# Samples in quarters, inputs first, and two weight places used once: a one-core trunk step with a mixture of experts

## What is computed

```python
x = _layernorm(x, ln_in_g, ln_in_b)
mix, C, n, m, S = _mixer(x, C_in[l], n_in[l], m_in[l], S_in[l], w_in[l], ...)
...
h = jnp.concatenate([h_a, h_b], axis=-1).astype(x.dtype)
return h @ w_out_l, C, n, m, S
```

## Time and profile before

| | us |
|---|---|
| median of the runs | 1262.06 |
| profiled execution, in all | 1263.85 |
| its span, first to last instruction | 1262.0 |
| TensorE matmul busy | 1166.6 (92%) |
| VectorE busy | 400.7 (32%) |
| ScalarE busy | 178.2 (14%) |
| GpSimd busy | 77.2 (6%) |
| mean granted TensorE clock | 0.976 |
| bytes moved | 441.92 MB, 350 GB/s over the span |

### The profile page before, as it was taken

One profiled execution on the slowest core, in us unless ns is written; L12 is line 12 of the kernel. 1 busy time (PEld: TensorE's weight loads), 2 busy tenths in 40 slices (PEclk: granted clock), 3 DMA queues, 4 the chain that ended last, 5 costly groups with the idle time before them and its releaser, 6 DMA issues.

```text
span 1262.0 us, 13214 instructions
## 1 busy us (share of the span) xinstructions
PE 1166.6 (92%) x5599; PEld 483.0 (38%) x5599; DVE 400.7 (32%) x643; ACT 178.2 (14%) x321; POOL 77.2 (6%) x77
## 2 busy tenths in 40 slices
PE   3999999799999997899999999999999999998984
PEld 2777774643333332242333333332323232322221
DVE  6866423841223130112322222232323222214115
ACT  1253242411010110020101010100101010110001
POOL 3100141400101030000000000000000000000000
PEclk9999999899999998999999999999999999999987
DMA  9562111579999999999999999999999999999891
GB/s 313 176 180 67 67 68 67 208 300 420 421 421 421 422 420 386 421 422 421 416 422 421 421 421 421 406 422 420 421 420 421 420 422 412 422 421 413 370 420 55
DMA packets 70029, 441.92 MB, mean 350 GB/s; under 512 B 7824, under 2 KB 7856, under 8 KB 20816
## 3 DMA queue, kind: packets, MB, share of 16 engines
q1 hardware_dynamic: 65168, 425.52, 82.6%
q0 software_dynamic: 4800, 15.51, 3.7%
HBM read 436.28 MB, written 4.73 MB: 349 GB/s over the span
## 4 chain that ended last, share of the span: by engine, by line
PE 70%; DMA 19%; DVE 8%; ACT 2%; issue 1%; SPq 1%; DVEq 0%
PE ps L935 41%; DMA more<-in_w_up 11%; PE ps L543 9%; PE ps L919 5%; PE ps L871 3%; DVE y_s L1740 2%; PE ps L761 2%; DMA ring<-in_w_gate 2%; DMA more<-in_w_down 2%; DMA more<-in_w_gate 2%; PE ps L926 1%; PE ps L571 1%; DVE h_s L1738 1%; ACT hTe L1084 1%; DMA ring<-in_w_up 1%; PE ps L951 1%
## 5 line engine op out<-in xcount | busy, mean ns | idle before, releaser
L935 PE MATMUL ps<-ring,xTe 128*64 128x512 f32 x1536 | 357.4, 602 | 13.4 <-DMA ring<-in_w_up 9.1
L935 PEld LDWEIGHTS ps<-ring,xTe 128*64 128x64 f32 x1536 | 103.9, 136 | 242.0 <-issue 241.8
L1722 DVE TENSOR_TENSOR xs<-xs,ps 128x512 f32<-128x512 f32 (+1 forms) x128 | 70.5, 551 | 365.3 <-PE ps L919 364.7
L935 PE MATMUL ps<-ring,hTe 128*64 128x512 f32 x768 | 181.4, 613 | 4.5 <-DMA ring<-in_w_down 4.5
L935 PE MATMUL ps<-more,xTe 128*64 128x512 f32 x512 | 117.1, 598 | 6.0 <-DMA more<-in_w_up 5.8
L543 PE MATMUL ps<-xT,ring 128*128 128x288 f32 x448 | 116.6, 417 | 1.0 <-PE ps L543 0.6
L935 PEld LDWEIGHTS ps<-ring,hTe 128*64 128x64 f32 x768 | 51.7, 139 | 119.7 <-issue 119.4
L543 PEld LDWEIGHTS ps<-xT,ring 128*128 128x128 f32 x448 | 85.8, 196 | 25.6 <-issue 2.3
L919 PE MATMUL ps<-y_s,GT 128*128 128x512 f32 (+1 forms) x256 | 81.8, 518 | 1.2 <-ACT y_s L1084 1.2
L1738 DVE TENSOR_SCALAR h_s<-ps 128x512 f32<-128x512 f32 x32 | 21.8, 681 | 159.3 <-PE ps L935 159.3
L1754 DVE TENSOR_TENSOR ple<-ple,ps 128x512 f32<-128x512 f32 (+1 forms) x64 | 35.3, 551 | 105.0 <-PE ps L871 90.8
(11 more groups left out here) (344 smaller groups left out, 796.2 us busy)
## 6 DMA issues: line engine op xcount, KB each, us to landing
ring<-in_w_gate SPq DMA_DIRECT2D x96, 1024.0 KB, 10.7
ring<-in_w_up SPq DMA_DIRECT2D x96, 1024.0 KB, 12.1
ring<-in_w_down SPq DMA_DIRECT2D x96, 1024.0 KB, 13.6
more<-in_w_gate SPq DMA_DIRECT2D x32, 1024.0 KB, 12.2
more<-in_w_up SPq DMA_DIRECT2D x32, 1024.0 KB, 12.1
more<-in_w_down SPq DMA_DIRECT2D x32, 1024.0 KB, 13.8
ring<-in_w_in SPq DMA_DIRECT2D x28, 512.0 KB, 6.1
ring<-in_w_out SPq DMA_DIRECT2D x8, 512.0 KB, 5.0
```

The lines of the kernel that those rows point to most:

```text
L935: last = mm(ps[64 * q:64 * q + 64, bank0 + half, :], lhs(k, q), wide(t)[:, k % 2, half * 512:(half + 1) * 512], start=False, stop=k == KT - 1)
L1722: last = tt(xs[0:r, i, c], xs[0:r, i, c], new, ALU.add)
```

## The change

- *Samples in quarters.* The samples' tile becomes `xq`, [128, 256]: partition 32q + t has quarter q of sample t. Its adds, statistics, normalisations and the share of the embeddings are done in that form. Statistics of the four quarters have to be brought together: VectorE spreads them with a mask (`spread_stats`) and TensorE multiplies by a matrix that is one where partitions agree modulo 32 (`row_stats`). Gains are loaded once more in quarters, eight small loads each time. The router product of the samples runs on a copy of them repeated four times (`xT4`), the selection on all 128 partitions. The bf16 parts of the samples are made in quarters, by ScalarE and VectorE, and put back into rows by 12 small products (`sample_rows`).
- *Inputs first.* SyncE loads all of x, then the first columns of the constants (the identity), then the gains; the other constants follow the first group of w_in. GpSimd's first loads wait until x is in. The statistics of all tiles are taken ahead of the wait for the gains.
- *Order.* `x1` stays in natural order (the router weights are loaded to match, in pieces of 128 bytes), and the reordering is done by ScalarE in `part` and by GpSimd in `rest`. TensorE does the prompt's part of the ranks ahead of the samples' rows, and both prompt-state blocks behind the ranks. The first `OH` is made in halves. The first six outputs on GpSimd's queue go ahead of its state operations, and those wait for the use of tile 8.
- *Places.* `once0` lies over `T1` and `T2`, `once1` over `V`. Tiles 8 and 9, the first two up tiles of pair 0, go there; from tile 10 on the eight places rotate as before, two tiles later. Tiles 10 to 17 wait for the use of tiles 0 to 7.
- *End.* The last `add_shares` takes a tile's statistics as soon as its adds are done.

The diff, cut to its core:

```diff
-PLACES = (0, 1, 2, 3, 4, 5, 6, 7)
-NWIDE = len(PLACES)
+NWIDE, NONCE = 8, 2
...
-        xs = sb("xs", [P, 3, D])
+        xs, xq = sb("xs", [P, 2, D]), sb("xq", [P, QW])
+        lnq, ln_q = sb("lnq", [P, 4, 6]), sb("ln_q", [P, 2, QW])
...
+        once = [nc.alloc_sbuf_tensor_at(f"once{n}", [P, 2, D], F32, offset=place[b][0]) for n, b in enumerate(("T1", "V"))]
...
+        def place_of(t):
+
+
+            return t if t < NWIDE + NONCE else (t - NONCE) % NWIDE
...
+            for i in range(2):
+                sp.dma_start(xs[:, i, :], x_src[i]).then_inc(S[f"x_in{i}"], 16)
+            for q, x in enumerate(quarters(x_src[2])):
+                sp.dma_start(xq[q * NS:(q + 1) * NS, :], x).then_inc(S["x_in2"], 16)
+            sp.dma_start(cf[:, 0:CF_FIRST], a["const_f"][:, 0:CF_FIRST]).then_inc(S["ident_in"], 16)
+            for n, v in enumerate(("ln_in_g", "ln_in_b")):
+                sp.dma_start((ln_g, ln_b)[n][:, :], a[v].partition_broadcast(P)).then_inc(S["ln1_in"], 16)
+                for q in range(4):
+                    sp.dma_start(ln_q[q * NS:(q + 1) * NS, n, :],
+                                 a[v][q * QW:(q + 1) * QW].partition_broadcast(NS)).then_inc(S["ln1_in"], 16)
...
+                if t < NWIDE + NONCE:
+                    if t == 6:
                         return sp.wait_ge(S["x_norm"], 6)
-                    if place_n == 7:
+                    if t == 7:
                         return sp.wait_ge(S["router_mm"], 3)
-                    return sp.wait_ge(S["slots_used"], range(2 * place_n + 1, PRE, RING)[-1] + 1)
-                p, u = divmod(t - NWIDE, PER)
+                    if t == 8:
+                        return sp.wait_ge(S["out_mm"], 6)
+                    if t == 9:
+                        return sp.wait_ge(S["st_mm"], 2)
+                    return sp.wait_ge(S["slots_used"], range(2 * t + 1, PRE, RING)[-1] + 1)
+                p, u = divmod(t - NWIDE if t >= 2 * NWIDE + NONCE else t - NWIDE - NONCE, PER)
...
+            for n, c0 in enumerate(W_GROUPS):
+                if n == 1:
+                    sp.dma_start(cf[:, CF_FIRST:], a["const_f"][:, CF_FIRST:]).then_inc(S["const_in"], 16)
...
+            pool.wait_ge(S["x_in2"], 64)
...
+                load_quarters("ln1_g", "ln1_b")
...
-                nc.gpsimd.tensor_tensor(out, out if q else x1[0:r, i, :], p, ALU.subtract).then_inc(S["rest_ok"], 1)
-
-            for i in range(3):
+                out = rests[:, i, :]
+                nc.gpsimd.tensor_tensor(natural(out), natural(out if q else x1[:, i, :]), by_row(xb[:, i, q, :]),
+                                        ALU.subtract).then_inc(S["rest_ok"], 1)
...
+            for i in range(2):
                 for q in range(2):
                     rest(i, q)
...
-            pool.wait_ge(S["out_mm"], 6)
...
+            pool.wait_ge(S["slots_used"], PRE + KT - 2 + 1)
...
+            pool.wait_ge(S["x_norm"], 6)
+            load_quarters("ln2_g", "ln2_b")
...
+            def row_stats(n):
+
+                pe.wait_ge(S["lnq_ok"], n)
+                mm(ps[:, STAT_BANK, 0:24], cf[:, CF_SAME:CF_SAME + P], lnq[:, :, :].rearrange("p q s -> p (q s)"),
+                   start=True, stop=True).then_inc(S["lnq_mm"], 1)
...
                 for k in range(KT):
-                    last = mm(ps[0:r, ROUTE_BANKS[i], 0:NE], xT[:, k, t0:t0 + r], w_r[:, k, :],
-                              start=k == 0, stop=k == KT - 1)
+                    x = xT[:, k, t0:t0 + r] if i < 2 else xT4[:, k, :, :].rearrange("p q t -> p (q t)")
+                    last = mm(ps[:, ROUTE_BANKS[i], 0:NE], x, w_r[:, k, :], start=k == 0, stop=k == KT - 1)
...
+            def prompt_ranks():
+
+
+                pe.wait_ge(S["pick_ok"], 2)
+                for i in range(2):
+                    for j in range(i + 1):
+                        rank(i, j, tri if j == i else ones, pick[:, j, :], NE)
+                for j in range(2):
+                    rank(2, j, ones, pick[:, j, :].unsqueeze(1).to_broadcast([P, 2, NE]), 2 * NE)
+
+            def sample_ranks():
+                pe.wait_ge(S["pick_ok"], 3)
+                rank(2, 2, cf[:, CF_TRI4:CF_TRI4 + P], pick[0:NS, 2, :], NE)
+                mm(ps[:, RANK_BANK, P + 3 * NE:P + 4 * NE], ones[0:NS, :], pick[0:NS, 2, :],
+                   start=False, stop=True).then_inc(S["rank_mm"], 1)
...
+            def sample_rows():
+
+                pe.wait_ge(S["partq_ok"], 3)
+                pe.wait_ge(S["logits_ok"], 2)
+                for q in range(4):
+                    for n in range(3):
+                        last = mm(ps[n * NS:(n + 1) * NS, ROW_BANKS[q // 2], (q % 2) * QW:(q % 2 + 1) * QW],
+                                  ident_b[:, q * NS:(q + 1) * NS], xbq[:, n, :], start=True, stop=True)
+                    if q % 2:
+                        last.then_inc(S["row_mm"], 1)
...
             project_out(2)
+            transpose_normed(1)
+            row_stats(2)
             route(0)
-            transpose_normed(1)
+            transpose_normed(2)
             route(1)
+            route(2)
+            prompt_ranks()
+            sample_rows()
+            sample_ranks()
             prompt_states_b()
-            transpose_normed(2)
-            route(2)
...
+            prompt_states_a()
...
-            pe.wait_ge(S["xT_ok"], 12)
-            prompt_states_a()
-            ranks()
-            pe.wait_ge(S["part_ok"], 9)
-            pe.wait_ge(S["OH_ok"], 1)
+            pe.wait_ge(S["part_ok"], 8)
+            pe.wait_ge(S["OH_first"], 1)
...
+                    f(by_row(xb[:, i, q, :]), natural(rests[:, i, :] if q else x1[:, i, :]), ACT.Copy).then_inc(S["part_ok"], 1)
...
+            def copy_sample_rows():
+                for n in range(2):
+                    act.wait_ge(S["row_mm"], n + 1)
+                    f(by_row(xb_s[:, :])[:, 64 * n:64 * n + 64, :], natural(ps[0:3 * NS, ROW_BANKS[n], :]),
+                      ACT.Copy).then_inc(S["part_ok"], 1)
...
+            copy_xT(2, 6, 0)
             part(1, 1)
-            part(2, 0)
-            part(1, 2)
-            copy_xT(2, 6, 0)
             part(2, 1)
             part(2, 2)
+            part(1, 2)
+            copy_sample_rows()
...
+            def spread_stats():
+
+                tt(lnq[:, :, :], lns[:, 2, 0:1, :].to_broadcast([P, 4, 6]),
+                   cf[:, CF_QUARTER:CF_QUARTER + 4].unsqueeze(2).to_broadcast([P, 4, 6]), ALU.mult).then_inc(S["lnq_ok"], 1)
...
+                if i == 2:
+                    dve.wait_ge(S["lnq_mm"], n // 3)
...
+                tile_stats(i)
+                if i == 2:
+                    dve.wait_ge(S["ident_in"], 16)
+                    spread_stats()
                 norm_stats(i, i + 1)
-                if i == 0:
-                    dve.wait_ge(S["ln1_in"], 32)
+            dve.wait_ge(S["ln1_in"], 160)
+            for i in range(3):
...
+                    dve.wait_ge(S["out_mm"], 6)
+                    stt(xq[:, :], xq[:, :], ALPHA, ps[:, 4, 0:QW], ALU.mult, ALU.add).then_inc(S["r1_ok"], 2)
...
+                    if after and n in (1, 3, 4):
+                        dve.wait_ge(S["cb_added"], p * 5 + (n + 1))
+                        after(i)
...
+            one_hot_half(0).then_inc(S["OH_first"], 1)
+            step(nc.vector.tensor_copy(ex[:, 3, :], ps[:, RANK_BANK, P + 3 * NE:P + 4 * NE]))
             selector(0, sel[0])
+            for i, (_, r) in enumerate(TILES):
+                ts(neg_v[0:r, i:i + 1], top_v[0:r, i, 0:1], -1.0, None, ALU.mult).then_inc(S["top_ok"], 1)
+            one_hot_half(1).then_inc(S["OH_ok"], 1)
+            dve.wait_ge(S["st_mm"], 3)
+            step(nc.vector.tensor_copy(np_s, ps[0:1, 3, 0:H * DKA]))
+            tt(n_old, n_old, ps[3 * NS:3 * NS + NSEQ, 3, H * DKA:2 * H * DKA], ALU.add).then_inc(S["n_ok"], 1)
...
+            add_shares(NPAIR - 1, tile_stats)
...
+            spread_stats()
```

More of the change, by code:

```diff
@@ L21 @@
 NS = NSEQ * TS
+QW = D // 4
 NT = NP + NS
@@ L103, in trunk_step, with quarters @@
     x_src = [a["x_prompt"][0, 0:P, :], a["x_prompt"][0, P:NP, :], a["x_sample"].rearrange("b t d -> (b t) d")]
+    def quarters(rows):
+        return [rows[:, q * QW:(q + 1) * QW] for q in range(4)]
     p_src = [a["p_prompt"][0, 0, 0:P, :], a["p_prompt"][0, 0, P:NP, :],
@@ L1076, in _ @@
                             combine_unit(n, GT[0])
+            row_stats(3)
         @block.scalar
@@ L1334, in _, with tile_stats @@
             nc.vector.memset(eps[:, 2:3], 1.0).then_inc(S["setup"], 1)
+            def tile_stats(i, done=None):
+                x = tokens(i)
+                for q in range(2 if i < 2 else 1):
+                    last = nc.vector.bn_stats(lns[:, i, q, :], x[:, q * 512:(q + 1) * 512] if i < 2 else x)
+                    (done or step)(last)
+            def spread_stats():
+                tt(lnq[:, :, :], lns[:, 2, 0:1, :].to_broadcast([P, 4, 6]),
```

(15 more changed lines are left out.)

274 lines of the change are left out of this document (138 added, 136 removed).

## The result

The changed kernel takes **1272.82 us** (median of four runs, 1272.39 to 1274.44) against 1261.93 of the kernel before: ratio 1.0085, 95% interval 1.0067 to 1.0102. It is 10.9 us slower, where 15.6 us less was forecast. The profiled execution has a span of 1270.6 us, 8.6 more than the one before.

What follows compares the result with a forecast made beforehand. The expert loop was taken as a weight stream at 419 GB/s, nearly balanced with TensorE, so savings ahead of it count fully. Terms 5.0 + 6.0 + 2.7 - 0.7 + 2.6 = 15.6 took 1262.06 to 1246.5 us, range 1240.0 to 1252.5.

Steps and rivals of the forecast that it cites:

- The middle term: Samples' out-projection to first expert product: that product at 250.2 instead of 256.17, 6.0 us earlier; ends 9.5 and 2.5.
- rival 2: Reordering on GpSimd costs there: prompt tile 1's subtractions collide longer with VectorE, 2.6 us later, 1249.1; chance 0.18.
- rival 5: Slower than before: step of eight far dearer on GpSimd's four subtractions; from 6.7 us each the 15.6 are gone; chance 0.03.
- Start: Kernel start to first projection: x loaded first, projection at 19.4 instead of 24.42, 5.0 us earlier; ends 2.0 and 6.3.
- Two tiles ahead: Expert weight stream: two tiles leave it, 5.0 us, less 2.3 of holes, leaving 2.7 us; ends 0 and 5.0.
- Rival 1: Expert weight stream: the holes add up or the clock slows pair 0, nothing of 5.0 left, 1249.2; chance 0.16.
- The first hole: Weight queue early in the expert loop: it waits for a place that comes one step later, 1.2 us of hole.
- Bytes: Inside the weight stream: eight quarter loads of the last gains, 0.26 MB, cost 0.7 us; ends 0 and 1.2.
- End: After the last product: the samples' shorter adds, statistics and wide operations save 2.6 us; ends 1.5 and 3.2.
- the collision with GpSimd: Before the first expert product: GpSimd's tile 1 subtractions delay VectorE; samples ready at 232.0, not 230.7, second selection loses 2.

Runs made afterwards that it cites:

- e1_undo: Changed kernel with VectorE again writing the prompt's normalised tiles in the experts' column order, so ScalarE's copies and GpSimd's subtractions are contiguous; 1259.65 us.
- e2_ends: Changed kernel with contiguous ScalarE writes, first quarter gains issued by ScalarE's queue, and last statistics of tiles 1 and 2 behind the branch; 1260.24 us.
- e3_best: Changed kernel with VectorE reordering the prompt's tiles, contiguous sample copies, tile 1's subtractions on VectorE, states early, gain loads on ScalarE's queue, branch value read early; 1254.23 us.

## Why the prediction was wrong

**The middle term, forecast 6.0, came as -12.7.** The step that failed stands in it unwritten: ScalarE's copies have no price. The prediction names them only in rival 2 ("copies and subtractions read or write with a step of eight") and then prices the subtraction alone; rival 5 speaks of ScalarE's queue, but counts there only what GpSimd takes and the 0.75 that VectorE's faster write gives back. In fact the copy cost 4.75 instead of 1.06, and the subtraction 2.86 instead of 2.12, where rival 2 had 3.4 (one of the four took 3.63, starting beside an operation of VectorE). By the Trainium skill, GPSIMD Engine Reference, Performance pitfalls for Q7 kernels, it would have been 3.2, the estimate in rival 2; the trace is below it. Nor is it a step of eight: the read is in order and the write jumps by 128 elements. I bounded GpSimd's cost by a VectorE row (2.0 against 1.27) and should have carried the same question to each engine that got the pattern. No row of before showed ScalarE with a strided write, so its upper end was open, and it belonged into the range.

The mechanism of rival 5 was right and its engine wrong. Its working, with ScalarE's numbers: three copies longer by 3.7, two subtractions by 0.75, less 2.07 to spare and 0.75 from the write, is 9.8 us for tile 0. In the rows the key copies start 5.66 us behind the end of the out-projection, where before they started 4.43 ahead of it: 10.1. Its chance of 0.03 rested on "Nothing in the trace shows a factor above 1.6", which was a statement on VectorE.

The rest of this term, with the copies contiguous: 2.6 (e1_undo) of 6.0. The states could begin 15.9 us behind the out-projection, 3.0 later than forecast (240.2 less 227.35), with the router products mostly at the lower clock level; they took 6.4 us, where I took 5.5; gathering and copy took 4.0 of my 4.5. That the states go better into TensorE's waits, worth some 4 us with the clock, I had not seen: I priced them at the place that the change gave them.

**Start, 5.0 forecast, 3.0 came,** and 2.3 of them at the first projection (22.09 for 24.42). The ten gain loads ended at 8.6 as forecast, but the last landed at 12.87 instead of "10.5 to 12", and transposes and copies took 2.3 us instead of 1.2. The w_in tiles were in time.

**Two tiles ahead, 2.7 forecast, 0.** Rival 1, in substance. The first hole came where forecast, at tile 18 (issued at 291.22, 25.3 behind the first product as before), and the lead fell by 2.1 up to tile 23, where I had 1.2. I expected the next at tile 26, with 2.5 of the lead left behind it. It came at tile 24 already (issued at 309.75) and took 1.8, and tile 26 took the rest. I had looked at one tile of that round and counted what was left as a gain; but every tile cuts the lead to what its own issue allows, and the lead has to last until TensorE waits for tiles, in pair 3.

**Bytes, -0.7.** Not told apart: with the two tiles the loop came out at 983.0 against 983.1.

**End, 2.6 forecast, 1.0.** The operations shrank as said. What the working lacks is the branch behind the last adds. Before, the samples' four adds of 0.41 covered it: there is no idle time between 1246.58 and the statistics:

```profile
1246.61 1.42 DVE L1341 BATCH_NORM_STATS2 lns<-xs 128x6 f32<-128x512 f32 x2
```

The change shortened these four to one and made the sequencer wait for each statistic, and 1.54 us came out from under them. This is the one place where I saved time on a cover without asking what it hid.

**Right:** the loop's stretch is still a stream of 416 GB/s; durations of the quarter-wide operations that met no subtraction (0.42 to 0.48); the collision with GpSimd; the place of the first hole; and that rivals 1 and 5 name, in kind, what came. The measured 1272.82 lies far outside 1240.0 to 1252.5.

## What to carry to other kernels

When a change moves a reordering to another engine, price the pattern on that engine, write and read apart, and try both loop orders: the same copy cost 4.75 or 2.07 us. A dear operation costs most through what stands behind it in its queue, here a square root of 0.28 us. And before a cover is shortened, or a lead is counted as a gain, look for what it hides and for where it is spent.

## What the runs showed of the hardware that I had not expected

- ScalarE, f32 to bf16, 1024 values a partition: 1.06 us with both sides in order, 2.07 with the read in steps of eight, 4.75 with the write in steps of 128. From PSUM, 512 values: 0.59 with the read in steps of eight, 2.4 to 2.8 with the write in steps of 128. The number of partitions (32 or 128) made no difference.
- The same strided write on VectorE took 2.45 us. GpSimd's subtraction with one input read in steps of 128 took 2.86 instead of 2.12. So each of these three engines pays for steps, and ScalarE for the write most of all. By the Trainium skill, SBUF — State Buffer, Specifications (TRN2), a 16-byte line needs at least two accesses for the full rate; the direction agrees, but by that rule alone ScalarE's write and its read, both in steps wider than a line, would cost alike, and 4.75 against 2.07 says that they don't.
- An operation of VectorE that takes 0.17 us by itself took 2.87 beside a subtraction on GpSimd, to whose end it was held. Not every one is held: a reciprocal of 0.16 us beside such a subtraction (at 240.62 in the changed kernel, the subtraction from 239.51 to 242.36) took its usual time.
- Reading a value and not taking the branch on it cost 1.5 us on VectorE's queue when nothing covered it (1.54 in the changed kernel, 1.09 idle and an add of 0.42 in e2_ends); with the value read ahead, at most 0.6 (0.19 idle and an add of 0.42, e3_best). The 1.3 us of TensorE in e3_best are put down to the same, which no run tested. By the Trainium skill, Advanced Engine Details and Errata, Control Flow Timing, a compare-and-branch is about 0.1 us; no row here shows the jump by itself.
